# Attention over chosen keys on Trainium2: scores of head pairs on both row halves, with deeper rings

## The reference, cut to what matters

```python
_, idx = lax.top_k(sc, topk)                       # topk = 256
valid = idx <= qpos[None, :, None]
ks = gather(k, idx)
vs = gather(v, idx)
att = jnp.einsum('bqhd,bqkd->bqhk', qb, ks).astype(f32) * (HEAD_DIM ** -0.5)
att = jnp.where(valid[:, :, None, :], att, -jnp.inf)
probs = jax.nn.softmax(att, axis=-1).astype(vs.dtype)
return jnp.einsum('bqhk,bqkd->bqhd', probs, vs)
```

## Time and profile before

| | |
|---|---|
| median of 3 runs | 3896.36 us (3893.3 to 3897.6) |
| profiled execution, first to last instruction | 3894.3 us, mean granted TensorE clock 0.966 |
| stage `dsa_attend` in layer 0 | 2006.5 to 2129.3 us, 122.8 us |
| stage `dsa_attend` in layer 1 | 3197.0 to 3319.5 us, 122.5 us |
| TensorE busy in the stage | 112.75 of 122.8 us |
| VectorE, ScalarE, GpSimd busy in it | 65.4, 54.7, 16.3 us |

### The profile page before, as it was taken

How to read it: one execution, slowest core, us unless ns; L and a number is a source line. 1 busy time by engine, 2 the same in 40 slices (tenths; PEclk the granted TensorE clock), 3 DMA queues, 4 the chain that set the end, 5 groups by cost and what they waited for, 6 DMA issues and landing times. The chain is left out here.

```text
span 3894.3 us, 57708 instructions
## 1 busy us (share of the span) xinstructions
PE 3592.1 (92%) x22944; PEld 2279.3 (59%) x22944; DVE 2153.7 (55%) x4617; ACT 1119.8 (29%) x2473; POOL 483.5 (12%) x304
## 2 busy tenths in 40 slices
PE   7999759799999997999998888998999999898898
PEld 5464434685478544655666776444655656787444
DVE  3244466446764574489965663342389965664333
ACT  2211254220122111320124555222230114555222
POOL 0020023000100010003221211110002221211110
PEclk9999879899999998999999999998999999999999
DMA  7432422334533343112341204111112340313320
GB/s 245 141 112 78 151 79 73 112 98 154 188 112 109 144 164 112 43 59 77 108 142 48 77 23 170 50 66 46 40 49 83 99 156 23 101 36 109 100 75 22
DMA packets 234285, 377.17 MB, mean 97 GB/s; under 512 B 30743, under 2 KB 163871, under 8 KB 233015
## 3 DMA queue, kind: packets, MB, share of 16 engines
q1 hardware_dynamic: 234030, 373.58, 28.9%
HBM read 290.84 MB, written 69.08 MB: 92 GB/s over the span
## 5 line engine op out<-in xcount | busy, mean ns | idle before, releaser
L3555 PE MATMUL win_acc<-across_room,across_hT 128*128 128x384 f32 (+3 forms) x3072 | 908.5, 456 | 3.7 <-PEq L83 3.7
L3555 PEld LDWEIGHTS win_acc<-across_room,across_hT 128*128 128x128 f32 x3072 | 561.4, 191 | 345.4 <-issue 15.5
L2611 DVE TENSOR_SCALAR_CACHE_REDUCE win_over<-d_sc,win_mid 128x384 uint8<-128x384 f32 (+5 forms) x384 | 337.9, 943 | 24.9 <-DVE win_mid L2622 24.5
L3394 PE MATMUL tail_wo<-tail_w_out,across_room 128*128 128x512 f32 x512 | 228.9, 601 | 9.3 <-issue 9.3
L3616 ACT ACTIVATE layer_spare<-win_acc 128x384 f32<-128x384 f32 (+1 forms) x144 | 67.2, 467 | 575.4 <-PE win_acc L3555 575.4
L491 PE MATMUL zin_acc<-zin_wt,across_hT 128*128 128x512 f32 (+2 forms) x640 | 229.2, 513 | 0.0
L3405 PE MATMUL tail_wg<-tail_w_gate,across_room 128*128 128x512 f32 x512 | 226.5, 597 | 1.0 <-DVE across_room L3235 1.0
L491 PEld LDWEIGHTS zin_acc<-zin_wt,across_hT 128*128 128x128 f32 x640 | 119.9, 190 | 98.3 <-issue 88.6
L3394 PEld LDWEIGHTS tail_wo<-tail_w_out,across_room 128*128 128x128 f32 x512 | 97.6, 193 | 128.2 <-issue 128.2
L1728 PE MATMUL mlp_bk<-across_hT,across_room 128*128 128x256 f32 x768 | 171.0, 379 | 0.0
L3405 PEld LDWEIGHTS tail_wg<-tail_w_gate,across_room 128*128 128x128 f32 x512 | 96.9, 192 | 117.3 <-issue 117.3
(11 more groups left out here) (526 smaller groups left out, 6593.4 us busy)
## 6 DMA issues: line engine op xcount, KB each, us to landing
across_room<-in_w SPq DMA_DIRECT2D x96, 1024.0 KB, 6.9
across_room<-in_w_in SPq DMA_DIRECT2D x18, 1536.0 KB, 8.6
s_z<-layer_spare SPq DMA_DIRECT2D x14, 1536.0 KB, 6.5
across_room<-in_w_ada SPq DMA_DIRECT2D x8, 2048.0 KB
across_hT<-s_z SPq DMA_DIRECT2D x16, 832.0 KB, 5.3
win_zp<-layer_spare SPq DMA_DIRECT2D x8, 1344.0 KB
zin_wt<-in_w_in SPq DMA_DIRECT2D x4, 2048.0 KB, 9.2
tail_w_out<-in_w_out SPq DMA_DIRECT2D x4, 2048.0 KB, 10.7
```

Source lines behind the costliest of these rows:

```text
L2611: s.put(dve.tensor_scalar(over[q][:, :], sc[q][:, :], mid[:, q:q + 1], 0.0, ALU.is_gt, ALU.add, accum_out=cnt[:, q:q + 1]))
L3394: mm = pe.matmul(wo[:, c, :], yT[:, n % 2, q, :], W["out"][:, q, c * COL:(c + 1) * COL], start=q == 0, stop=q == KC - 1)
L3555: mm = pe.matmul(acc[:, u % RING, 0:w], hT[:, k, t * P:(t + 1) * P], wt[:, i % 2, k, 0:w], start=k == 0, stop=k == KC - 1)
```

## The change

- Scores of two heads (a pair p, 16 in all) are issued together: for each 512 columns first the head on rows 0 to 63, then the head on rows 64 to 127, each in its own `acc` bank. They wait once, until both heads of the pair before were masked.
- `att` has 4 buffers in place of 3, `pT` 4 in place of 2. `values` follows two groups behind `turn` in place of one (`LAG = 2`).
- ScalarE does `exps(m + 2)` after the copies of step m in place of `exps(m + 1)` ahead of them.
- The four pieces of `choose` for tile 7 stand in a row after step 1; those for tile 6 begin after steps 3 and 5. `rows_out` of the tile before moves from head 1 to head 3 of a tile.
- Fills: 16 at the start, then 2, 2, 2 and 8 after pairs 0 to 3; 30 in all.
- Pieces of `Opening`: `O1` stands before the scores of pair 13, and VectorE's pieces come one step later (table `DVE_AT`), with two left for after the last `rows_out` where one was.

```diff
-        att = ph.sb("att", [P, 3, SEQ])
+        att = ph.sb("att", [P, 4, SEQ])
-        pT = ph.sb("pT", [P, 2, 4, P])
+        pT = ph.sb("pT", [P, 4, 4, P])
...
+        LAG = 2
...
-                def scores(m):
-                    t, h = TILE_ORDER[m // DSA_H], m % DSA_H
+                def scores(p):
+                    t = TILE_ORDER[p // 2]
                     L = (t + 1) * P
-                    pr = slice(64 * (h % 2), 64 * (h % 2) + 64)
-                    if m >= 2:
-                        pe.wait_ge(masked, START + m - 1)
+                    if p >= 1:
+                        pe.wait_ge(masked, START + 2 * p)
                     for c in range(0, L, COL):
                         w = min(COL, L - c)
-                        mm = pe.matmul(acc[:, m % 2, c // COL, 0:w], B["qT"][pr, h // 2, t * P:(t + 1) * P], B["kT"][pr, c:c + w], start=True, stop=True)
+                        for h in range(2):
+                            pr = slice(64 * h, 64 * h + 64)
+                            mm = pe.matmul(acc[:, h, c // COL, 0:w], B["qT"][pr, p % 2, t * P:(t + 1) * P], B["kT"][pr, c:c + w], start=True, stop=True)
                     mm.then_inc(made, 1)
...
-                def busy_after(m):
-                    i, h = m // DSA_H, m % DSA_H
-                    if i < 2 and h < DSA_H - 1:
-                        keep_busy(i % 2, 8 if m == 2 * DSA_H - 2 else 2)
-
                 scores(0)
-                scores(1)
                 keep_busy(0, 16)
                 opening = O.tensor(pe)
                 k = 0
-                for m in range(NM):
-                    if m + 2 < NM:
-                        scores(m + 2)
-                    while k < len(groups) and groups[k][0] == m:
-                        turn(k)
-                        if k >= 1:
-                            values(k - 1)
-                            if groups[k - 1][0] != m:
-                                busy_after(m - 1)
-                        k += 1
-                    if m in (LATE, LATE + 1, LATE + 2):
-                        if m == LATE:
+                for p in range(NM // 2):
+                    if LATE // 2 <= p < LATE // 2 + 3:
+                        if p == LATE // 2:
                             pe.wait_ge(masked, START + LATE)
                         next(opening)
-                values(k - 1)
+                    if p + 1 < NM // 2:
+                        scores(p + 1)
+                    while k < len(groups) and groups[k][0] // 2 == p:
+                        turn(k)
+                        if k >= LAG:
+                            values(k - LAG)
+                        k += 1
+                    if p < DSA_H:
+                        keep_busy(p // 2, 8 if p == DSA_H - 1 else 2)
+                for q in range(len(groups) - LAG, len(groups)):
+                    values(q)
...
-                DVE_AT = {1: 1, 2: 1, 3: 2, 4: 1, 5: 3}
+                DVE_AT = {2: 1, 3: 1, 4: 1, 5: 2, 6: 1, 7: 1}
...
                     attend(m)
-                    if not (i == 1 and h < 2):
+                    if m == 1:
+                        for _ in range(4):
+                            next(steps)
+                    if m in (3, 5) or i >= T0:
                         next(steps, None)
-                    if h == 1 and i >= 1:
+                    if h == DSA_H - 1 and i >= 1:
                         rows_out(i - 1)
...
                 exps(0)
+                exps(1)
                 k = 0
                 for m in range(NM):
-                    if m + 1 < NM:
-                        exps(m + 1)
                     while k < len(groups) and groups[k][0] == m:
                         take(k)
                         k += 1
+                    if m + 2 < NM:
+                        exps(m + 2)
```

More of the change, by code:

```diff
@@ L2696, in turn @@
                     for b in range(nb):
-                        mm = pe.transpose(tp[:, k % 2, b, :], att[:, m % 3, (b0 + b) * P:(b0 + b + 1) * P], ident[:, :])
+                        mm = pe.transpose(tp[:, k % 2, b, :], att[:, m % 4, (b0 + b) * P:(b0 + b + 1) * P], ident[:, :])
                     mm.then_inc(turned, 1)
@@ L2707, in values @@
                     for b in range(nb):
-                        mm = pe.matmul(po[:, i % 2, h * HD:(h + 1) * HD], pT[:, k % 2, b, :], B["v"][:, b0 + b, :], start=b0 + b == 0, stop=b0 + b == t)
+                        mm = pe.matmul(po[:, i % 2, h * HD:(h + 1) * HD], pT[:, k % 4, b, :], B["v"][:, b0 + b, :], start=b0 + b == 0, stop=b0 + b == t)
                     if h == DSA_H - 1 and b0 + nb == t + 1:
                         mm.then_inc(o_made, 1)
-                def busy_after(m):
-                    i, h = m // DSA_H, m % DSA_H
-                    if i < 2 and h < DSA_H - 1:
-                        keep_busy(i % 2, 8 if m == 2 * DSA_H - 2 else 2)
                 scores(0)
-                scores(1)
                 keep_busy(0, 16)
@@ L2792, in attend @@
                     dve.wait_ge(mask_ready, START + i + 1)
[L2793 to L2796, removed]
+                    dve.wait_ge(made, START + m // 2 + 1)
+                    if m >= 4:
+                        dve.wait_ge(turned, START + upto(m - 4))
+                    dve.tensor_tensor_reduce(att[:, m % 4, 0:L], acc[:, m % 2, :, :].rearrange("p a n -> p (a n)")[:, 0:L], mask[:, i % 2, 0:L],
                                              -float(HD) ** -0.5, BIG, ALU.add, ALU.min, nm[:, m:m + 1]).then_inc(masked, 1)
@@ L2832, in exps @@
                     t = TILE_ORDER[m // DSA_H]
-                    a = att[:, m % 3, 0:(t + 1) * P]
+                    a = att[:, m % 4, 0:(t + 1) * P]
                     act.wait_ge(masked, START + m + 1)
@@ L2839, in take @@
                     act.wait_ge(turned, START + k + 1)
-                    act.activation(pT[:, k % 2, 0:nb, :], tp[:, k % 2, 0:nb, :], ACT.Copy).then_inc(pT_ready, 1)
+                    act.activation(pT[:, k % 4, 0:nb, :], tp[:, k % 2, 0:nb, :], ACT.Copy).then_inc(pT_ready, 1)
                 opening = O.scalar(act)
                 exps(0)
+                exps(1)
                 k = 0
                 for m in range(NM):
-                    if m + 1 < NM:
-                        exps(m + 1)
                     while k < len(groups) and groups[k][0] == m:
```

## The result

The changed kernel takes 3844.89 us (median of 4 runs, 3843.14 to 3850.13), the kernel before 3895.36 beside it: a ratio of 0.9871, 95% interval [0.9859, 0.9883]. That is 50.5 us less. The forecast was 3850.4 in a range of 3840 to 3868, with "faster" at 0.94.

A forecast was written before the change was run, and what follows sets the result against it. TensorE bounds the kernel, busy 3592 of 3894 us; the stage's end is bound by hand-offs. Body 15, start 6 and end 2 make 23 us a layer, 46 in both: 3850.4 us, range 3840 to 3868.

The forecast's parts named there:

- Two row halves at one time: Scores throughout the stage: matmuls on rows 0 to 63 and 64 to 127 overlap, so a pair costs one head.
- The body, 15: Stage's TensorE-bound middle, 61.2 us: 11.9 saved on scores and 4.0 on waits, less 0.9, per layer.
- the 0.9 us for a late VectorE: Taken off the middle's saving because VectorE would now and then be some tenths late; bounds 0 and seven times 1 us.
- slack of 0.6 us in tile 6: Masking path of about 4.2 us fits beside TensorE's 4.8 us of transposes and values by 0.6.
- The waits of `values`, 4.0: Stage's middle: 4.0 us of waits, mostly for ScalarE's copy, go with two groups of lag and four `pT` buffers.
- The start, 6: From the opening fills' end to the first long transposes: 21.5 us becomes 15.1, saving 6 per layer; bounds 1.8 and 8.
- The end, 2: Stage's hand-off-bound last 30.3 us: shorter scores against added values and opening work, saving 2 per layer; bounds -2.3 and +5.
- VectorE as the loop: Rival: scores and masking alternate, each of 12 long pairs loses about 0.7 us; gain 15 a layer, 3866 us; chance 0.22.
- No overlap: Rival: the row halves do not run at once; gain eight a layer, 3880 us; chance 0.04.
- The clock falls in the body: Rival: half clock in the stage's middle costs 38 us, net +15 a layer, 3926 us; chance 0.03.
- more is won: Rival: start 8, body 16 and end 5, a gain of 29 a layer, 3838 us; chance 0.10.
- the marks named for "wrong": Stage: halves in sequence, TensorE waiting 0.5 us for `datt_nm` before each pair, clock under 0.9 before the end, end 30 us.

The follow-up runs named there:

- doubling run: Changed kernel with both heads of a pair on rows 0 to 63: 3876.51 us, 0.9954 of the kernel before.

## Why the prediction was right, point by point

**Two row halves at one time: right**, and the sum hung on it. The doubling run shows it from the other side, 13.1 us a layer when it is taken away, as worked out.

**The body, 15: it was 17.3.** The saved scores are right: the seven pairs take 10.0 us from their first weight load to the next transposes, 9.9 were worked out. Two terms were mis-sized. Transposes and values take 43.8 - 10.0 = 33.8 us for 104 blocks, 0.325 a block and not 0.34 (1.6 us). And the 0.9 us for a late VectorE was not needed: nothing of `datt_nm` is among the body's waits. The slack of 0.6 us in tile 6 was real; it was 0.9 to 1.0 (the second masking ends at 2043.41 and 2049.85, the next scores begin at 2044.58 and 2051.11, of which some 0.25 is the hand-off). It was closest one pair earlier: masked at 2037.19, scores at 2037.60, 0.2 to spare. VectorE was busy 34.05 of 43.8 us, 78%, where "three quarters" was named.

**The waits of `values`, 4.0: right in size.** With one group of lag the body gets 4.3 us back, 3.1 of them in waits for the copy. But transposes and values with all their waits took 39.3 us of the body before (61.1 less 21.8), 38.0 in the run with one group of lag and 33.8 now. So 1.2 us came off by something other than the lag. Pairing, which leaves half as many changes between scores and transposes, and ScalarE's new order are candidates; no run tells them apart.

**The start, 6: it was 6.4**, the worked-out 15.1 to the tenth. That it came out to the tenth was luck, for the reason was only half right. The prediction added up TensorE's instructions, the fills among them, as if they set the end of the part. The run without the small fills is no shorter: the first long masking, a running sum and the second long masking must be done before the second long pair. In the kernel after the eight fills come out even with that chain (a wait of 0.33 for `datt_nm` at 2031.30), so both sums give the same. They were costed as TensorE time, 3.7 us and four fewer for 1.8, and should have been named as cover. The mask of tile 7 "ready near 2019" was off as well, though harmless. `choose` is done at 2017.03, but GpSimd is asked only after step 3's masking:

```profile
2019.36 2.36 POOL L2756 TENSOR_TENSOR across_room<-across_room 128x1024 f32<-128x1024 f32 x1 [8.84 <-DVE datt_nm L2793]
2021.81 1.76 POOL L2757 TENSOR_SCALAR across_room<-across_room 128x1024 f32<-128x1024 f32 x1
```

It is ready at 2023.6, and the first long masking begins at 2026.62.

**The end, 2: it was 0.5 in layer 0 and 4.3 in layer 1**, within the bounds. That the wait of 2.44 us stays was right (2.45, below). The 1.3 for more values behind the last transposes and the piece after the last `rows_out` are there too: the last value instructions take 3.94 us for 18, where the earlier trace rows had 2.66 for 12. What the term left out is that the clock decides most of the part's size, and that it need not fall. Timeline of the end in layer 0 of the kernel after, then of the same place in layer 1 of the same execution:

```profile
2083.35 0.30 PEld L2690 LDWEIGHTS datt_acc<-d_kT,d_qT 64*128 64x128 f32 x4 [2.45 <-DVE datt_nm L2793]
...
2088.25 0.55 PEld L1959 LDWEIGHTS datt_acc<-layer_spare,layer_early 128*128 128x128 f32 x2
```
```profile
3247.27 0.30 PEld L2690 LDWEIGHTS datt_acc<-d_kT,d_qT 64*128 64x128 f32 x4 [2.44 <-DVE datt_nm L2793]
...
3250.68 0.30 PEld L1959 LDWEIGHTS datt_acc<-layer_spare,layer_early 128*128 128x128 f32 x2
```

The same wait, and then 4.90 us to `O3` in layer 0, 3.41 in layer 1. Windows give the clock, first of layer 0's end, then of layer 1's from that wait on:

```profile
2077.00:2083.40 6.40, 4.47 (x33) 2.84 (x31) 2.42 (x7) 3.05 (x10) 1.51 (x2) 1.00 0.00 0
2083.40:2084.90 1.50, 1.50 (x11) 0.95 (x11) 0.85 (x2) 1.48 (x3) 0.00 (x0) 1.00 0.00 0
2084.90:2091.00 6.10, 6.10 (x24) 4.57 (x22) 2.45 (x7) 2.04 (x4) 0.00 (x0) 0.52 0.06 21
2091.00:2098.00 7.00, 5.10 (x36) 3.96 (x35) 5.35 (x14) 5.76 (x13) 0.00 (x0) 0.93 0.01 2
2098.00:2103.70 5.70, 4.63 (x21) 4.45 (x21) 0.01 (x1) 1.84 (x5) 0.00 (x0) 0.57 0.07 23
```
```profile
3247.30:3250.70 3.40, 3.40 (x28) 2.85 (x29) 1.75 (x5) 2.83 (x5) 0.00 (x0) 1.00 0.11 39
3250.70:3256.00 5.30, 4.96 (x32) 3.39 (x31) 4.38 (x13) 3.44 (x9) 0.00 (x0) 1.00 0.01 3
```

The half-clock stretch does not fall in the wait but behind it, on work that is needed. Over all runs with this end untouched it took 28.5 to 31.9 us: three ends of 28.5 or 28.6 at a mean clock of 0.82 to 0.84, eleven of 30.2 and more at 0.72 to 0.77. Their mean is 30.6, against 32.2 in the two layers before. So the end gains 1.6 us a layer in the mean, and the forecast of 2 was well sized; the 4.3 of layer 1 was luck.

**The rivals.** VectorE as the loop: not in the body, by the waits above; it is the loop in the start. No overlap: excluded. The clock falls in the body: 1.00 throughout. What was won over the forecast is a little of the "more is won" case, by the body more than by start and end. Of the marks named for "wrong" one came, an end of 30 us or more (30.4 in its window), in one layer.

**The sum.** 46 us forecast, 50.6 measured in the stages: 4.6 from the body, 0.8 from the start, 0.8 from the end (less 1.5, and 2.3 more), less 1.6 for layer 1's opening fills, which took 9.2 us where they took 7.6 before. The prediction had no term for those.

## What to carry to other kernels

Where a contraction fills half the rows, issue two independent ones on the two halves into two banks; here that was worth 13 us of a stage of 123 in its start and body, and the order of issue did not matter. Matmuls that fill a gap cost nothing as long as another engine's chain is longer, so find that chain and shorten it before you take fills away. In a tail of hand-offs, price each stop of TensorE twice, the wait and the slower work behind it; eight idle matmuls in those stops saved 4.4 us of 31.

## What the runs showed of the hardware that I had not expected

- With all instructions of head 0 issued ahead of head 1, the two row halves still ran side by side: eight instructions in 1.99 us, body 43.84 against 43.80. The Trainium skill has matmuls start in program order ("TensorE: Matmul & The Clock Gate", Part 3, "The mechanism"). By that only the middle two of the four chunks would have overlapped, an estimated 0.9 us more for this pair (one chunk of 512 columns at 0.215 us for 128). No such time shows, so here the measurement decides against it.
- The granted clock fell to its lower level after waits shorter than the 2.4 us that the rows of before suggested: in the window from 2098 to 2103.7 above it is 0.57, behind two waits with little work between them. And it did not always fall after 2.44 (layer 1 above). The two waits in the kernel after's timeline, with the three transposes behind the second taking 0.50 us to load, 0.31 behind the first:

```profile
2096.58 0.31 PEld L2699 LDWEIGHTS datt_tp<-layer_ident,datt_att 128*128 128x128 f32 x3 [1.78 <-ACT datt_att L2835]
...
2099.02 0.50 PEld L2699 LDWEIGHTS datt_tp<-layer_ident,datt_att 128*128 128x128 f32 x3 [1.41 <-ACT datt_att L2835]
```

- The opening fills, the same 32 instructions, took 9.2 us in some stages and 7.6 in others, and 24 of them 5.8 or 7.5. The shorter case is 0.23 us an instruction, the full-clock price of the earlier trace rows; the longer holds 1.7 us more. That is the clock again: windows of the opening in the kernel after and in the run with one head after the other, both in layer 0 and both behind the same 2.40 us without a weight load:

```profile
2008.80:2018.10 9.30, 9.23 (x38) 7.53 (x38) 6.73 (x10) 2.16 (x5) 1.62 (x4) 0.82 0.79 213
```
```profile
2005.50:2013.10 7.60, 7.50 (x36) 6.33 (x36) 6.06 (x10) 2.16 (x5) 1.62 (x4) 1.00 0.65 177
```
